# Last stage of a one-core kernel: half of each token's expert rows summed by TensorE through diagonal gate matrices, normalization and stores in two halves

## What is computed

```python
gate = gate / jnp.sum(gate, axis=-1, keepdims=True) * ROUTED_SCALE
routed = routed_experts(h, idx, gate, w_gate, w_up, w_down)   # per token: sum over its 8 experts of gate * row
shared = (jax.nn.silu(h @ ws_gate) * (h @ ws_up)) @ ws_down
...
x = x + g2 * (routed + shared)
...
y = x32 * lax.rsqrt(jnp.mean(x32 * x32, axis=-1, keepdims=True) + EPS)   # rmsnorm, EPS = 1e-6
return (y * g.astype(F32)).astype(x.dtype)
```

## Time and profile before

| what | us |
|---|---|
| median of 3 runs | 5573.13 (5566.98 to 5587.94) |
| the profiled execution: its own time | 5573.14 |
| its span | 5570.9 |
| start of the last stage's first gather in the span | 5423.40 |
| last VectorE sum of the last stage starts | 5530.3 |

### The profile page before, as it was taken

One profiled execution on the slowest core, in us unless ns is written; L12 is line 12 of the kernel. 1 busy time (PEld: TensorE's weight loads), 2 busy tenths in 40 slices (PEclk: granted clock), 3 DMA queues, 4 the chain that ended last, 5 costly groups with the idle time before them and its releaser, 6 DMA issues. The chain is left out here.

```text
span 5570.9 us, 75850 instructions
## 1 busy us (share of the span) xinstructions
PE 4536.2 (81%) x29164; PEld 2951.7 (53%) x29164; DVE 1700.5 (31%) x2707; ACT 1093.8 (20%) x1593; POOL 877.3 (16%) x619
## 2 busy tenths in 40 slices
PE   7999757769997996577799877779778999999972
PEld 3666646656665885365566545553534444444431
DVE  1000555542412007455514224431221111111117
ACT  1001232321222113222212232220201111111110
POOL 1111012212222210221122200000041000000005
PEclk9999877779998998677899976669789999999985
DMA  4334222222212221100022100001108888888867
GB/s 163 151 151 158 78 84 100 85 78 87 80 64 81 93 79 63 42 21 21 32 79 87 57 25 4 4 15 40 64 1 323 316 318 323 315 316 312 322 240 256
DMA packets 156860, 714.48 MB, mean 128 GB/s; under 512 B 25697, under 2 KB 27490, under 8 KB 132578
## 3 DMA queue, kind: packets, MB, share of 16 engines
q1 hardware_dynamic: 106498, 536.10, 26.9%
q0 software_dynamic: 24512, 81.84, 4.3%
q10 hardware_dynamic: 25632, 93.33, 4.1%
HBM read 584.23 MB, written 126.98 MB: 128 GB/s over the span
## 5 line engine op out<-in xcount | busy, mean ns | idle before, releaser
L400 PE MATMUL ps<-s_proj_hS,s_proj_wS 128*128 128x512 f32 x3216 | 761.2, 398 | 62.4 <-POOL s_proj_wS L312 62.4
L2586 PE MATMUL ps<-s_exp_gu,keep_hT 128*128 128x512 f32 x1472 | 690.9, 625 | 104.0 <-DMA s_exp_gu<-in_w_gu_dram 103.0
L400 PEld LDWEIGHTS ps<-s_proj_hS,s_proj_wS 128*128 128x128 f32 x3216 | 605.0, 189 | 223.3 <-ACT s_proj_wS L361 63.3
L2586 PEld LDWEIGHTS ps<-s_exp_gu,keep_hT 128*128 128x128 f32 x1472 | 285.9, 199 | 451.2 <-issue 403.0
L1727 PE MATMUL ps<-s_mix_hS,s_mix_wS 128*128 128x512 f32 x1536 | 393.9, 412 | 38.6 <-POOL s_mix_wS L1586 33.0
L1727 PEld LDWEIGHTS ps<-s_mix_hS,s_mix_wS 128*128 128x128 f32 x1536 | 290.6, 190 | 133.9 <-issue 65.8
L1586 POOL TENSOR_TENSOR s_mix_wS<-s_mix_w,s_mix_wS 128x1024 fp32r<-128x1024 f32 x96 | 230.7, 2404 | 685.5 <-ACT s_mix_wS L1595 685.5
L2570 PE MATMUL ps<-s_exp_wd,s_exp_aT 128*128 128x512 f32 x736 | 332.9, 595 | 1.9 <-ACT s_exp_aT L2496 1.9
L2536 DVE TENSOR_TENSOR s_exp_sg<-s_exp_sg,ps 128x256 f32<-128x256 f32 x92 | 38.7, 421 | 786.6 <-ACT s_exp_sg L2517 786.6
L312 POOL TENSOR_TENSOR s_proj_wS<-s_proj_w,s_proj_wS 128x1024 fp32r<-128x1024 f32 x67 | 162.7, 2433 | 689.1 <-ACT s_proj_wS L361 689.1
L340 DVE COPY s_proj_o<-ps 128x512 f32<-128x512 f32 x66 | 45.6, 692 | 706.3 <-PE ps L400 706.3
(11 more groups left out here) (441 smaller groups left out, 6504.1 us busy)
## 6 DMA issues: line engine op xcount, KB each, us to landing
s_exp_gu<-in_w_gu_dram SPq DMA_DIRECT2D x92, 2048.0 KB
s_exp_wd<-in_w_down_dram SPq DMA_DIRECT2D x92, 1024.0 KB
yrow<-keep_hT ACTq DMA_DIRECT2D x92, 512.0 KB, 11.1
s_proj_wa<-in_w_ada_dram SPq DMA_DIRECT2D x72, 512.0 KB, 4.3
s_proj_w<-in_w_in_dram SPq DMA_DIRECT2D x66, 512.0 KB
proj<-s_proj_o ACTq DMA_DIRECT2D x66, 512.0 KB
yrow<-keep_xT SPq DMA_DIRECT2D x4, 8192.0 KB
s_mix_w<-in_w_in_dram SPq DMA_DIRECT2D x64, 512.0 KB
```

The lines of the kernel that those rows point to most:

```text
L400: mm = pe.matmul(k.ps[:, 6 + half if last else 2 * b + half, :], wS[:, b, x, t, :], hS[:, y, t, half * HALF:(half + 1) * HALF], start=(t = ...
L2586: mm = pe.matmul(k.ps[:, 2 if u == 0 else 6, :], xT[:, u, t, :], gu[:, u, t, :], start=(t == 0), stop=(t == KT - 1))
```

## The change

Only `combine` is rewritten.

- Experts j = 0 to 3 (NSUM = 4) of a tile are summed by VectorE as before. For experts 4 to 7 ScalarE makes a diagonal matrix `dg` of the gates (`k.eye` times the gate, one activation of 128x128 each, 4 for a tile, two tiles' worth of `dg`), and TensorE multiplies the gathered rows by it. The product is the gate-weighted tile already transposed. The transposes of `acc` become matmuls with `k.eye` that add to the same PSUM region. For each of the 8 column groups there are 4 matmuls with `dg` and one with `k.eye`.
- TensorE starts a tile when the tile's 8 gathers have landed and its 4 sums are done.
- There are NBUF = 12 buffers. The gathers of a tile come in the order 0, 4, 1, 5, 2, 6, 3, 7 (`TURN`), so VectorE's and TensorE's rows alternate. A buffer of TensorE's is free when TensorE has finished that whole tile (`turned`).
- The squares are made tile by tile by ScalarE (one activation of 128x1024 into `sq`), and their sums by TensorE (8 matmuls of 128x128 for tile i-1, behind the matmuls of tile i).
- Ln, Exp, the final multiplication and the stores are done for tokens 0 to 511 (`normalized(0)`, on VectorE between tiles 6 and 7) and again for tokens 512 to 1023. There are 16 stores of 256 KB.

```diff
-    NBUF = 6
+    NBUF = 12
+    NSUM = TOPK // 2
+    TURN = [j for s in range(NSUM) for j in (s, NSUM + s)]
...
+        def place(i, j):
+            return i * TOPK + TURN.index(j)
...
-                for j in range(TOPK):
-                    n = i * TOPK + j
+                for j in TURN:
+                    n = place(i, j)
                     if n >= NBUF:
-                        pool.wait_ge(summed, n - NBUF + 1)
+                        before, who = (n - NBUF) // TOPK, TURN[(n - NBUF) % TOPK]
+                        if who < NSUM:
+                            pool.wait_ge(summed, before * NSUM + who + 1)
+                        else:
+                            pool.wait_ge(turned, before + 1)
...
             for i in range(NTT):
-                pe.wait_ge(summed, (i + 1) * TOPK)
+                pe.wait_ge(dg_ready, i + 1)
+                for j in range(NSUM, TOPK):
+                    n = place(i, j)
+                    pe.wait_ge(ld_y[n % NBUF], 16 * (n // NBUF + 1))
+                pe.wait_ge(summed, (i + 1) * NSUM)
                 if i >= 2:
                     pe.wait_ge(x_ready, i - 1)
                 for t in range(KT):
-                    tr = pe.transpose(k.ps[:, 2 * (i % 2) + t // 4, (t % 4) * P:(t % 4 + 1) * P], acc[:, i, t * P:(t + 1) * P], k.eye[:])
-                tr.then_inc(turned, 1)
+                    turn = k.ps[:, 2 * (i % 2) + t // 4, (t % 4) * P:(t % 4 + 1) * P]
+                    for j in range(NSUM, TOPK):
+                        pe.matmul(turn, y[:, place(i, j) % NBUF, t * P:(t + 1) * P], dg[:, i % 2, j - NSUM, :], start=(j == NSUM), stop=False)
+                    mm = pe.matmul(turn, acc[:, i, t * P:(t + 1) * P], k.eye[:], start=False, stop=True)
+                mm.then_inc(turned, 1)
+                if i:
+                    sums(i - 1)
+            sums(NTT - 1)
...
+            diagonals(0)
+            diagonals(1)
+            for i in range(NTT):
+                squares(i)
+                if i + 2 < NTT:
+                    diagonals(i + 2)
+                if i == NTT // 2:
+                    deviations(0)
+            deviations(1)
```

More of the change, by code:

```diff
@@ L2601, in combine @@
     acc = k.mix
-    NBUF = 6
+    NBUF = 12
+    NSUM = TOPK // 2
+    TURN = [j for s in range(NSUM) for j in (s, NSUM + s)]
     with Stage(k, "comb") as s:
         y = s.sb("y", [P, NBUF, D])
+        dg = s.sb("dg", [P, 2, TOPK - NSUM, P])
+        sq = s.sb("sq", [P, 2, KT, P])
         fg, rstd = s.sb("fg", [P, KT]), s.sb("rstd", [P, T])
         ld_y = [s.sem(f"ld_y{b}") for b in range(NBUF)]
-        names = "ld_g summed turned x_ready sq_ready ss_ready own_a rstd_ready o_ready st_o"
-        (ld_g, summed, turned, x_ready, sq_ready, ss_ready, own_a, rstd_ready, o_ready, st_o) = (s.sem(n) for n in names.split())
+        names = "ld_g dg_ready summed turned x_ready sq_ready ss_ready own_a rstd_ready o_ready st_o"
+        (ld_g, dg_ready, summed, turned, x_ready, sq_ready, ss_ready, own_a, rstd_ready, o_ready, st_o) = (s.sem(n) for n in names.split())
         block = s.block()
+        def place(i, j):
+            return i * TOPK + TURN.index(j)
         @block.sync
@@ L2613, in _ @@
             sp.dma_start(fg[:], I["final_g"]).then_inc(ld_g, 16)
[L2614 to L2617, removed]
+            for h in range(2):
+                for j in range(KT):
+                    sp.wait_ge(o_ready, h * KT + j + 1)
+                    sp.dma_start(k.out[j, :, h * HALF:(h + 1) * HALF], k.hT2[:, j, h * HALF:(h + 1) * HALF]).then_inc(st_o, 16)
+            sp.wait_ge(st_o, 32 * KT)
         @block.gpsimd
@@ L2636, in to_residual, with normalized @@
                 ins.then_inc(x_ready, 1)
+            def normalized(h):
+                dve.wait_ge(rstd_ready, h + 1)
+                dve.wait_ge(x_ready, (h + 1) * NTT // 2)
+                w = slice(h * HALF, (h + 1) * HALF)
+                for j in range(KT):
+                    dve.scalar_tensor_tensor(k.hT2[:, j, w], k.xT[:, j, w], fg[:, j:j + 1], rstd[:, w], ALU.mult, ALU.mult).then_inc(o_ready, 1)
+            dve.wait_ge(ld_g, 16)
             for i in range(NTT):
-                for j in range(TOPK):
-                    n = i * TOPK + j
+                for j in range(NSUM):
+                    n = place(i, j)
                     dve.wait_ge(ld_y[n % NBUF], 16 * (n // NBUF + 1))
                     if j:
-                        dve.wait_ge(summed, n)
+                        dve.wait_ge(summed, i * NSUM + j)
                     dve.scalar_tensor_tensor(acc[:, i], y[:, n % NBUF, :], k.gates[:, i, j:j + 1], acc[:, i],
@@ L2647, in _, with sums @@
                     to_residual(i - 1)
+                if i == NTT - 2:
+                    normalized(0)
             to_residual(NTT - 1)
[L2649 to L2653, removed]
+            normalized(1)
         @block.tensor
         def _(pe):
-            for i in range(NTT):
-                pe.wait_ge(summed, (i + 1) * TOPK)
+            def sums(i):
+                pe.wait_ge(sq_ready, i + 1)
+                for t in range(KT):
+                    mm = pe.matmul(k.ps[:, 4 + i // 4, (i % 4) * P:(i % 4 + 1) * P], k.ones[:], sq[:, i % 2, t, :],
+                                   start=(t == 0), stop=(t == KT - 1))
+                mm.then_inc(ss_ready, 1)
+            for i in range(NTT):
+                pe.wait_ge(dg_ready, i + 1)
+                for j in range(NSUM, TOPK):
+                    n = place(i, j)
+                    pe.wait_ge(ld_y[n % NBUF], 16 * (n // NBUF + 1))
+                pe.wait_ge(summed, (i + 1) * NSUM)
                 if i >= 2:
@@ L2669, in _ @@
-            mm.then_inc(ss_ready, 1)
+                    turn = k.ps[:, 2 * (i % 2) + t // 4, (t % 4) * P:(t % 4 + 1) * P]
[5 more added lines that the diff above has]
+                    sums(i - 1)
@@ L2671, in _, with diagonals @@
+            sums(NTT - 1)
         @block.scalar
         def _(act):
[L2673 to L2679, removed]
+            def diagonals(i):
+                if i >= 2:
+                    act.wait_ge(turned, i - 1)
+                for j in range(NSUM, TOPK):
+                    ins = act.activation(dg[:, i % 2, j - NSUM, :], k.eye[:], ACT.Copy, scale=k.gates[:, i, j:j + 1])
+                ins.then_inc(dg_ready, 1)
@@ new lines, in squares, with deviations @@
+            def squares(i):
+                act.wait_ge(x_ready, i + 1)
+                if i >= 2:
+                    act.wait_ge(ss_ready, i - 1)
+                act.activation(sq[:, i % 2], k.xT[:, :, i * P:(i + 1) * P], ACT.Square).then_inc(sq_ready, 1)
+            def deviations(h):
+                w = slice(h * HALF, (h + 1) * HALF)
+                act.wait_ge(ss_ready, (h + 1) * NTT // 2)
+                act.activation(rstd[:, w], k.ps[:, 4 + h, :], ACT.Ln, scale=1.0 / D, bias=EPS).then_inc(own_a, 1)
+                act.wait_ge(own_a, h + 1)
+                act.activation(rstd[:, w], rstd[:, w], ACT.Exp, scale=-0.5).then_inc(rstd_ready, 1)
```

## The result

The changed kernel took 5613.20 us (median of 6 runs, 5597.44 to 5621.73), the kernel before 5574.31 us (median of 6, 5560.19 to 5587.94). The ratio is 1.0069, 95% interval 1.0048 to 1.0090: slower by 0.7%, 38.9 us by the medians.

The account below looks back on a forecast made before the run. VectorE was taken as the bound before, a loop of GpSimd, gathers and TensorE after: 5450.1 plus 7 x 19.7 plus 17.8 ends at 5605.8, +34.9 us, added to 5573.1 for 5608 us; range 5587 to 5626.

Parts of the forecast that it names:

- first gather to turned(0): First tile: eight gathers without a wait end at 5438.9, TensorE needs 9.0 + 2.2 us, so its tile ends at 5450.1.
- gathers of a turn, from GpSimd's first issue to TensorE's start: Between tiles: three gathers issued and landed, 8.0 us, plus about 0.1 us for TensorE to start.
- TensorE's tile and the step from it to GpSimd's issue: 80 instructions, 9.0 us at full clock plus 2.4 for the cold start; GpSimd sees the semaphore after about 0.2 us.
- a turn: One round from one tile's TensorE end to the next: 8.3 + 9.0 + 2.4 = 19.7 us, against 12.99 before.
- behind the last turn: Residual, squares, sums, Ln, Exp, eight multiplications and the last stores after TensorE's last tile: 17.8 us.
- The bound before: In the old kernel's tile, VectorE barely sets the pace; freeing it gives at most about 1.4 us a tile, 11 us in all.
- The loop: In the buffer ring, a tile's last three gathers wait for TensorE's previous whole tile, and TensorE waits for them: 19.7 us a turn.
- The landing of three gathers: Term of each turn: three gathers into idle DMA queues take 8.0 us, from the stage's first three gathers.
- the 7 to 9 us that the prediction named as its sign: Time from `turned` to the next tile's first matmul; any other value would mean the prediction was wrong in size.
- The cold start: After some 6.5 us idle, TensorE starts each tile at half clock for 5.1 us, which costs 2.4 us a tile.
- The end: Work behind the last turn: 17.8 us in sum, with 5.1 for eight multiplications and 4.3 to the end of the span.
- The open ring as a rival: Rival: GpSimd runs ahead, the DMA rate bounds the stage, device time 5552 us, 5541 at 400 GB/s; chance 0.06.

Follow-up runs that it names:

- the series 10, 12, 14, 16: The changed kernel with 10, 14 or 16 buffers in place of 12: stage 207.3, 158.5 and 138.9 us, against 185.4.
- release by gather: The changed kernel, 12 buffers, each TensorE buffer freed after its own 16 instructions, TensorE starting at a tile's first gather: 5511.76 us, ratio 0.9948 to the kernel before.
- the five sums: The changed kernel released gather by gather, 16 buffers, VectorE summing five of eight experts, TensorE three: stage 123.3 us, ratio 0.9955 to the kernel before.

## Why the prediction was right

By its own steps:

| step | predicted, us | measured, us |
|---|---|---|
| first gather to turned(0) | 26.7 | 26.4 (5427.54 to 5453.95) |
| gathers of a turn, from GpSimd's first issue to TensorE's start | 8.1 | 8.6 (8.0 to 9.3) |
| TensorE's tile and the step from it to GpSimd's issue | 11.4 + 0.2 | 11.7 (11.4 to 12.0) |
| a turn | 19.7 | 20.3 |
| seven turns | 137.9 | 142.4 |
| behind the last turn | 17.8 | 16.6 |
| the stage | 182.4 | 185.4 |
| against before | +34.9 | +37.9 |

- *The bound before* was VectorE, as said: twelve buffers alone gave nothing. What a faster VectorE could give was put too low, at 1.4 us a tile, since the DMA rate behind it was.
- *The loop* was read off the arithmetic n-12 and is shown by the series 10, 12, 14, 16 and, most plainly, by the order of gathers alone. It is enough to explain the loss: with the order alone changed the stage takes 146.5 us, a little less than before. With release by gather the same division of work is 31 us faster in the stage than before (116.2 against 147.5).
- *The landing of three gathers* was the term sized too low: 8.0 us taken from the start of the stage, where the measured 8.0 to 9.3 us in the seven turns hold, in two of them, VectorE's fourth sum as well. This makes most of the 4.5 us by which seven turns were longer than predicted. From `turned` to the next tile's first matmul it was 8.2 to 9.6 us, mean 8.9; two of the seven, 9.4 and 9.6, lie above the 7 to 9 us that the prediction named as its sign. The rule of the Trainium skill, "DMA: Bandwidth & Descriptors", section "Anatomy of one DMA — SWDGE (gpsimd) path", gave an estimate of 5.6 us; the measurement decides against it here.
- *The cold start* was put at 2.4 us a turn and is 2.3 in the mean, the changed kernel's tiles less the tile at full clock of the kernel with added work. The Trainium skill, "TensorE: Matmul & The Clock Gate", section "HAM oscillation — how this bites in real kernels", has bursts of matmuls that are parted by waits for DMA each start throttled, and the changed kernel's trace agrees: behind 6.5 to 8.6 us of idle time each tile starts at 0.50. It must not be read as a rule on short bursts as such: released by gather, with next to no idle time between them, they ran at 1.00.
- *The end* was 1.2 us too high: 8 multiplications of 512 columns took 5.39 us, costed at 5.1, but the stores of 256 KB ended 3.2 us behind them, where 4.3 had been taken for 512 KB, and what lies between the last turn and the multiplications took 8.0 us in place of 8.4. This error hides a part of the turns'.
- *The open ring as a rival* was priced at 5552 us, 22 us faster, for a ring that lets GpSimd run ahead and still turns whole tiles. The nearest run to it, 16 buffers, was 8.6 us faster in the stage, since GpSimd still waited every second tile. With release by gather the stage was 31 us shorter: TensorE then works while the gathers land and has only its last gather's matmuls and the identity's left, and the DMA rate reached 383 GB/s.

What stays open: how much of the five sums' longer stage is GpSimd's slower issues and how much VectorE's own queue at the end, which of the three full engines sets the pace with release by gather, and what besides the length of the idle time decides whether the clock falls.

## What to carry to other kernels

When a buffer's release moves from one engine to another, write down for each transfer which event it now waits for, and ask whether that event itself needs the transfer: a ring that holds one tile and a half, released by whole tiles, was a loop here, whose length is transfer latency plus compute, and no engine's busy share in the profile of before showed it. Release each buffer after its own last reader (116.2 us of stage here), or order the transfers so that those that wait for the slow release come first in a tile (146.5 us, against 185.4). And when a change has two halves, time each: here one was worth 13 us, and the other hid it by costing 51.

## What the runs showed of the hardware that I had not expected

- Added work made the loop shorter: 12 more matmul instructions a tile in TensorE's idle time took the stage from 185.4 to 175.8 us. In the turns at a granted clock of 1.00 a turn took 17.8 to 18.1 us with the added work, where it takes 20.3 without.
- Idle times of 2.62 and 2.78 us were followed by half clock, one of 3.61 us was not.
- The gathers of 4 KB rows can run at 383 GB/s over 67 us with the DMA engines' share at 1.00; before, at 91% share, they moved 329 GB/s, so rate over share understated the ceiling.
- Gathers are issued more slowly beside VectorE's sums. The 64 issues took 63.4 us in the changed kernel, where VectorE mostly waited, 68.6 and 71.4 with four sums a tile at full pace (12 and 16 buffers), 75.2 with five, and 76.9 and 73.5 with eight (6 and 12 buffers in the kernel before). The number of sums is not all that counts: the eight with 12 buffers are below the five.
- The sums of four column groups in one PSUM bank were kept open side by side, the bank being opened by one matmul of zeros of 512 columns (bf16, 0.41 us), 16 of them in the stage. No run leaves these out.
